# Hybrid projections: half of the modulation products move from VectorE to ScalarE and GpSimd, and their sums on TensorE one product later

## The reference, cut to what matters

```
def ada_modulation(cond, w, b):
    m = jax.nn.silu(cond) @ w + b
    return jnp.split(m, 6, axis=-1)
...
        sh1, sc1, gt1, sh2, sc2, gt2 = (t[:, None, :] for t in ada_modulation(c, ada_w[i], ada_b[i]))
        csh1, csc1, cgt1, csh2, csc2, cgt2 = ada_modulation(c_ctx, ada_w[i], ada_b[i])
```

## Time and profile before

| what | us |
|---|---|
| three timed runs | 3459.10, 3459.01, 3449.18 (median 3459.01) |
| the profiled execution | 3452.43 |
| its span, first to last instruction | 3450.6 |
| the stage in layer 0, first feature product to the end of the last row product | 43.07 to 294.61 |
| the stage in layer 1, the same | 495.49 to 743.30 |

### The profile page before, as it was taken

How to read it: one execution, slowest core, us unless ns; L and a number is a source line. 1 busy time by engine, 2 the same in 40 slices (tenths; PEclk the granted TensorE clock), 3 DMA queues, 4 the chain that set the end, 5 groups by cost and what they waited for, 6 DMA issues and landing times. The chain is left out here.

```text
span 3450.6 us, 72773 instructions
## 1 busy us (share of the span) xinstructions
PE 3102.1 (90%) x31974; PEld 1794.0 (52%) x31974; DVE 1645.8 (48%) x3491; ACT 784.3 (23%) x1863; POOL 313.3 (9%) x345
## 2 busy tenths in 40 slices
PE   6998999989799999599999979998888878698987
PEld 5854658646344565343333335557787765233332
DVE  3664635757464586411112154238887866322211
ACT  2103410125211372100000010136555541000000
POOL 0000000000011110000000000012332320000000
PEclk9998999999899999699999989999999998899999
DMA  6565125730311223599999922100000024699998
GB/s 181 148 206 160 26 80 143 206 111 26 112 64 43 74 67 122 199 371 391 389 389 392 351 85 73 43 1 5 4 5 4 5 109 180 253 409 410 417 410 350
DMA packets 136476, 605.34 MB, mean 175 GB/s; under 512 B 17409, under 2 KB 20033, under 8 KB 115553
## 3 DMA queue, kind: packets, MB, share of 16 engines
q1 hardware_dynamic: 131136, 583.38, 45.7%
q0 software_dynamic: 5024, 17.30, 2.1%
HBM read 578.50 MB, written 28.44 MB: 176 GB/s over the span
## 5 line engine op out<-in xcount | busy, mean ns | idle before, releaser
L2129 PE MATMUL psum<-ring,big 128*32 128x256 f32 (+1 forms) x2688 | 389.1, 496 | 19.6 <-issue 9.1
L2129 PE MATMUL psum<-front,big 128*32 128x256 f32 (+1 forms) x2384 | 320.0, 480 | 8.4 <-issue 4.2
L441 PE MATMUL psum<-h_uT,ring 128*128 128x264 f32 x1280 | 290.5, 387 | 0.0
L570 DVE SCALAR_TENSOR_TENSOR h_O<-h_O,cond_silu 128x512 f32<-128x512 f32 x336 | 227.1, 747 | 103.8 <-DMA h_O<-ada_w 103.8
L2129 PEld LDWEIGHTS psum<-ring,big 128*32 128x32 f32 (+1 forms) x2688 | 136.3, 124 | 262.0 <-issue 220.3
L441 PEld LDWEIGHTS psum<-h_uT,ring 128*128 128x128 f32 x1280 | 242.0, 190 | 46.5 <-issue 5.8
L2270 DVE TENSOR_TENSOR big<-big,psum 128x512 f32<-128x512 f32 (+1 forms) x48 | 28.8, 599 | 438.1 <-PE psum L2129 425.7
L2129 PEld LDWEIGHTS psum<-front,big 128*32 128x32 f32 (+1 forms) x2384 | 114.1, 122 | 206.0 <-issue 174.0
L2768 PE MATMUL psum<-ring,gates 64*64 64x128 f32 (+1 forms) x5120 | 171.7, 253 | 11.8 <-issue 10.0
L461 PE MATMUL psum<-ring,h_uT 128*128 128x512 f32 x384 | 169.3, 598 | 0.0
L2209 ACT ACTIVATE big<-psum 128x512 f32<-128x512 f32 (+1 forms) x48 | 23.5, 524 | 636.1 <-PE psum L2129 636.1
(11 more groups left out here) (454 smaller groups left out, 5118.0 us busy)
## 6 DMA issues: line engine op xcount, KB each, us to landing
ring<-moe_w SPq DMA_DIRECT2D x84, 2048.0 KB, 14.0
front<-moe_w SPq DMA_DIRECT2D x67, 2048.0 KB, 14.2
big<-moe_w SPq DMA_DIRECT2D x28, 2048.0 KB, 29.7
h_O<-ada_w SPq DMA_DIRECT2D x192, 256.0 KB, 2.9
ring<-w_in SPq DMA_DIRECT2D x16, 2048.0 KB, 13.1
X<-moe_w SPq DMA_DIRECT2D x13, 2048.0 KB, 12.5
ring<-na_w_qkv SPq DMA_DIRECT2D x6, 2048.0 KB, 8.1
ring<-w_out SPq DMA_DIRECT2D x4, 2048.0 KB, 9.2
```

The source lines that it names most:

```text
L441: last = nc.tensor.matmul(bank(k, pair_bank(q) + h, NH), w[:, a, f * P:(f + 1) * P], uT[:, a, halves[h]], start=a == 0, stop=a == KD - 1)
L570: nc.vector.scalar_tensor_tensor(into, ada(u), by, into, ALU.mult, ALU.add).then_inc(s.acc, 1)
L2129: last = nc.tensor.matmul(bank(k, b, r.width)[q * r.n:(q + 1) * r.n, :], rowsT[:, half * HALF_K + n, r.first:r.first + r.n], w[:, n, q * r ...
```

## The change

For the context's half, `weigh` on VectorE is dropped (it now does r = 0 alone, and `acc` counts one for a unit). ScalarE multiplies the unit's tile by the context's column into one of two small buffers (`ctx_part`, a free part of `X`), and GpSimd adds that buffer to the context's sum, or copies it there for the first unit of a chunk. ScalarE waits for the unit's load and, from the third unit on, for GpSimd's add two units back. It does so at a fixed place in its own queue: the units of place q are scaled before the copy-out of the product q+1, hence after the copy-out of product q. SyncE's load of the unit four later waits for VectorE and ScalarE. `mod_sum(n)` waits for VectorE's and GpSimd's counts, and `made` puts it after the product two places behind the last unit's, not one; `mod_out(n)` and the store move with it.

```diff
@@ mod_schedule
-                made.setdefault(q + 1, []).append(u // KD)
+                made.setdefault(q + 2, []).append(u // KD)
@@ hybrid_project
+    ctx_part = lambda u: k.X[:, LT + 1, u % 2 * CHUNK:(u % 2 + 1) * CHUNK]
@@ sync: load_unit
-                    sp.wait_ge(s.acc, 2 * (u - MOD_BUFS) + 2)
+                    sp.wait_ge(s.acc, u - MOD_BUFS + 1)
+                    sp.wait_ge(s.ctx_scaled, u - MOD_BUFS + 1)
@@ gpsimd
+            for u in range(MOD_UNITS):
+                n, a = u // KD, u % KD
+                into = acc(n)[:, 1, :]
+                pool.wait_ge(s.ctx_scaled, u + 1)
+                if a == 0:
+                    if n >= 2:
+                        pool.wait_ge(s.mod_summed, n - 1)
+                    nc.gpsimd.tensor_copy(into, ctx_part(u)).then_inc(s.ctx_acc, 1)
+                else:
+                    pool.wait_ge(s.ctx_acc, u)
+                    nc.gpsimd.tensor_tensor(into, into, ctx_part(u), ALU.add).then_inc(s.ctx_acc, 1)
@@ tensor: mod_sum
-                pe.wait_ge(s.acc, 2 * KD * (n + 1))
+                pe.wait_ge(s.acc, KD * (n + 1))
+                pe.wait_ge(s.ctx_acc, KD * (n + 1))
@@ scalar
+            def scale(u):
+                act.wait_ge(ada_here[u % MOD_BUFS], 16 * (u // MOD_BUFS + 1))
+                if u >= 2:
+                    act.wait_ge(s.ctx_acc, u - 1)
+                nc.scalar.activation(ctx_part(u), ada(u), ACT.Copy, scale=k.cond_silu[:, u % KD, 1:2]).then_inc(s.ctx_scaled, 1)
+
             for q, (kind, j) in enumerate(order):
+                for u in units[q - 1] if q else ():
+                    scale(u)
                 if kind == "mirror":
                     continue
@@ vector: weigh
-                for r in range(2):
-                    into, by = acc(n)[:, r, :], k.cond_silu[:, a, r:r + 1]
...
-                        dve.wait_ge(s.acc, 2 * u + r - 1)
-                        nc.vector.scalar_tensor_tensor(into, ada(u), by, into, ALU.mult, ALU.add).then_inc(s.acc, 1)
+                into, by = acc(n)[:, 0, :], k.cond_silu[:, a, 0:1]
...
+                    dve.wait_ge(s.acc, u)
+                    nc.vector.scalar_tensor_tensor(into, ada(u), by, into, ALU.mult, ALU.add).then_inc(s.acc, 1)
```

More of the change, by code:

```diff
@@ L353, in hybrid_project @@
     with ExitStack() as mem, stage(k, "product out_done mirror_out rope_step logits_out forget_act forget_dve lam_dve lam_act summed "
-                                      "ada_here0 ada_here1 ada_here2 ada_here3 gate_bias0 gate_bias1 acc mod_summed mod_out "
+                                      "ada_here0 ada_here1 ada_here2 ada_here3 gate_bias0 gate_bias1 acc ctx_scaled ctx_acc mod_summed mod_out "
                                       "row_stored0 row_stored1 cleared") as (block, s):
@@ L522, in _ @@
                 last.then_inc(s.out_done, 1)
+            for u in units[len(order) - 1]:
+                scale(u)
         @block.vector
@@ L563, in weigh @@
                 dve.wait_ge(ada_here[u % MOD_BUFS], 16 * (u // MOD_BUFS + 1))
-                for r in range(2):
-                    into, by = acc(n)[:, r, :], k.cond_silu[:, a, r:r + 1]
-                    if a == 0:
-                        nc.vector.tensor_scalar(into, ada(u), by, None, ALU.mult).then_inc(s.acc, 1)
-                    else:
-                        dve.wait_ge(s.acc, 2 * u + r - 1)
-                        nc.vector.scalar_tensor_tensor(into, ada(u), by, into, ALU.mult, ALU.add).then_inc(s.acc, 1)
+                into, by = acc(n)[:, 0, :], k.cond_silu[:, a, 0:1]
+                if a == 0:
+                    nc.vector.tensor_scalar(into, ada(u), by, None, ALU.mult).then_inc(s.acc, 1)
+                else:
+                    dve.wait_ge(s.acc, u)
+                    nc.vector.scalar_tensor_tensor(into, ada(u), by, into, ALU.mult, ALU.add).then_inc(s.acc, 1)
             def mod_out(n):
```

## The result

The changed kernel takes 3469.59 us in the median of 8 executions (3454.96 to 3473.48), the kernel before 3456.14 of 8 (3449.18 to 3459.10): a ratio of 1.0038 [1.0023, 1.0053], **slower by 13 us** where 3451.0 was forecast. The profiled execution took 3467.39 us, its span 3465.6.

What follows compares the result with a forecast made beforehand. TensorE was taken to bound both stages. From the profiled 3452.4 us, 5.5 of waits won and 1.0 left gave 3448.0, a gain of 4.5; off the executions' middle of 3455.7 that made about 3451, range 3444 to 3463.

Steps and rivals of the forecast that it cites:

- Moved: loads: Four-unit stretches: loads wait for ScalarE, chunk goes out at t0 + 4.5, copy-out ready at t0 + L + 12.4.
- the dear case: Late-unit path with GpSimd's add at 1.32 us and VectorE's operation at 1.51; the first two waits missed by 1.6 and 0.6.
- TensorE bounds, and only waits before sums count: Both stages: TensorE is the bound; its waits before sums cost 5.47 us together, all the change can win.
- ScalarE's added work is covered, late copies cost nothing: 96 scalings a layer at 0.63 us fit beside TensorE's products; a copy-out may be 14.4 us late before TensorE notices.
- GpSimd: 1.04 to 1.32 us an add: GpSimd's 84 adds and 12 copies: four take 4.2 to 5.3 us, covered by a row product of 7.0.
- VectorE's remaining half: VectorE's remaining operation may go from 0.69 to 1.51 us; 0.7 taken for the path, 1.5 kept for the range.
- L of 13.3 to 16.9: Time in us from a 2 MB chunk's issue to the arrival of the units queued behind it, from four measured pairs.
- Moved: the sum: Sum one product later, due 29.4 us after F15's end or 28.6 after F19's; TensorE waits only above L 17.0 or 16.2.
- With the dear values the ready time is 1.7 later: Copy-out behind late units with GpSimd's add at 1.32 us and VectorE's operation at 1.51: ready 1.7 us later.
- The end is free: End of each stage: the last sum, just before the last meta tile, costs nothing; 1.4 us a layer if stores land slowly.
- the wait only moves: Rival at the sums: TensorE waits one product later for as long as before; 3452 to 3459 us, chance 0.20.
- an engine becomes the bound: Rival at four-unit places: GpSimd (add above 1.78 us) or VectorE becomes the bound; about 3466 us at 1.90, chance 0.12.

Runs made afterwards that it cites:

- narrow_add2: The changed kernel with GpSimd's 84 adds a layer cut from 512 to 64 columns; median 3448.41 us, 0.9988 of the kernel before.
- vector_adds2: The changed kernel with GpSimd's copies and adds moved to VectorE, at the next place in the order; median 3461.66 us, 1.0023 of the kernel before.
- sum_later2: The kernel before with only its sums one product later, nothing moved to ScalarE or GpSimd; median 3452.87 us, 1.0004 of the kernel before.
- before again: The kernel before, unchanged, run once more for a second trace; median 3450.89 us, 1.0004 of the kernel before.
- after again: The changed kernel, unchanged, run once more for a second trace; median 3466.84 us, 1.0048 of the kernel before.
- out_first2: The changed kernel with VectorE's copy-out of a sum ahead of the same place's weighing; median 3459.70 us, 1.0033 of the kernel before.
- two_later_out_first: The changed kernel with sums one product later still and VectorE's copy-out ahead of the weighing; median 3456.95 us, 1.0022 of the kernel before.

## Why the prediction was wrong

**The step that failed is *Moved: loads*, in the part "the change, part by part"**: its term for working off the late units, from their arrival to the copy-out. I had the units of both places ahead of the copy-out, but let ScalarE, VectorE and GpSimd keep up with the loads, so that behind the last load there was one operation of 0.7 us, and came to 3.4 + 3.0 + 0.7 + 0.42 + 0.3, some 7.9 us. VectorE didn't keep up: its eight operations, 1.46 us each with GpSimd beside them, take 12.1 us with the copy-out (186.44 to 198.53). In the dear case I put 1.51 into the sum once, not eight times.

The rows above show which part was short. The fourth scaling ends at 190.29 + 0.72 = 191.01, 4.6 us after the units' arrival and not 3.4; with 3.0 for its load the last unit would be there near 194.0. At 193.94 VectorE still has three operations to do, 4.25 us and not 0.7. Had its operation stayed at 0.75 us, the same path would be 4.6 + 3.0 + 0.75 + 0.41 = 8.8 us. That is an estimate, but narrow_add2 comes to 9.0. By it some 3.3 of the 4.2 us that this term lacks are VectorE's slowing, and the rest the pace of GpSimd's adds, to which ScalarE is held. No run changes one without the other in this kernel, so the split is not shown.

The path of each kernel in layer 0, in us after the end of F15 (read as above: SyncE's chunk, VectorE's first late unit, the end of the copy-out, and TensorE's sum without its wait; the forecast's row has L = 16.9):

| kernel | chunk | L | worked off | copy-out done | sum due | wait |
|---|---|---|---|---|---|---|
| forecast | 4.5 | 16.9 | 7.9 | 29.3 | 29.4 | 0 |
| after | 5.8 | 16.4 | 12.1 | 34.3 | 30.1 | 4.34 |
| vector_adds2 | 4.6 | 15.8 | 9.8 | 30.1 | 30.1 | 0.20 |
| narrow_add2 | 3.7 | 15.5 | 9.0 | 28.1 | 30.0 | none |
| sum_later2 | 0.1 | 15.4 | 10.7 | 26.2 | 30.0 | none |

Of the forecast's miss of 5.0 us in "copy-out done", 4.2 are the working off, 1.3 the chunk (adds of 1.33 and scalings of 0.72, not 1.04 to 1.32 and 0.63), and L gives 0.5 back. Against sum_later2 the hybrid is 8.1 us later: 5.7 by the chunk, 1.0 by L, 1.4 by the working off. Narrowing the add takes back 6.1 of these and leaves 2.0, the net price of hanging the loads on ScalarE.

The second stretch, behind F19, inherits this. The pair of engines is still at the first one's units, so the chunk (205.30) goes out 11.0 us after F19's end instead of 4.5. The copy-out ends at 232.61, and the sum, due at 232.75 - 2.60 = 230.15 only because the first wait has already pushed it back, waits again.

By the prediction's other points:

- *TensorE bounds, and only waits before sums count.* Right. The floor was a little lower: 246.43, not 246.94, so that 6.5 us and not 5.47 could be won.
- *ScalarE's added work is covered, late copies cost nothing.* Right. The scaling took 0.72 for 0.63. F18's copy started at 190.92, 3.8 us after F18's end (half of 14.51 after 179.83), and TensorE did not notice.
- *GpSimd: 1.04 to 1.32 us an add.* Too low: 1.26 at least, 1.41 in the mean of layer 0 and of both layers. The row of 1.043 was the wrong neighbour; the one of 1.322 was right for an undisturbed add.
- *VectorE's remaining half: 0.7 for the path, "since GpSimd has its pauses when units are late".* Wrong, and the argument was upside down: late units arrive together, and behind them both engines have hardly a pause. The range of 1.5 was right for the place that counts.
- *L of 13.3 to 16.9.* Right: 16.4 and 15.2 (220.53 - 205.30).
- *Moved: the sum.* Two sums stand between t0 and the moved one, not one: it was due at t0 + 30.1, not 29.4, which is 0.7 us in the change's favour.
- *"With the dear values the ready time is 1.7 later."* By the prediction's own terms it is 2.0: 0.6 more for the chunk, 0.6 for the working off, 0.8 for VectorE. It changes no reading.
- *The end is free.* Right: TensorE's pause between the last meta tile and the next stage is 2.04 us after the change, 2.03 in sum_later2.
- *Rival "the wait only moves".* One of its conditions, the dear values, came true, and TensorE does wait one product later. But it let the waits stay as long as they were (3452 to 3459), and they grew. *Rival "an engine becomes the bound".* It named the right two engines, but asked whether they keep up with TensorE over a whole place (an add above 1.78 us). None has to: they need only be too slow once, in the queue behind a late transfer.

**What stays open.** The ratios put the loss at 13 to 17 us (I had expected 6 to 13 of after again), the stages at 9.4 and 9.9; some 4 to 7 us are not accounted for. The rest of the span varies by itself: behind the second stage it has 2707.3 us in before and 2716.8 in before again, 2718.3 and 2718.0 in the changed kernel's two traces, but 2708.4 in out_first2 and 2707.2 in two_later_out_first, which have the same work on ScalarE and GpSimd. This is the same stretch of layer 1's attention in before, before again and after (length; busy PE, PEld, DVE, ACT, POOL; clock, DMA share, GB/s):

```profile
743.30:850.00 106.70, 94.01 (x766) 67.72 (x767) 74.93 (x292) 64.33 (x191) 14.55 (x30) 0.95 0.07 24
```

```profile
735.20:847.00 111.80, 100.19 (x767) 71.96 (x764) 74.44 (x290) 64.46 (x191) 14.59 (x30) 0.86 0.07 22
```

```profile
747.30:858.00 110.70, 98.21 (x764) 70.69 (x765) 74.52 (x292) 64.38 (x191) 15.03 (x30) 0.90 0.08 23
```

The same matmuls keep TensorE busy for 94.0 us at a granted clock of 0.95 and for 100.2 at 0.86, and the kernel before stands at both ends. The first profile of before was the lucky one, so the difference of the two first spans, 15.0 us, overstates the change. What the change adds to the time outside its stages no run here has isolated.

## What to carry to other kernels

When an instruction is moved in a program, write down what stands ahead of it on every engine at its new place, and price the whole queue behind a late transfer, not the last instruction in it: engines that are idle half of the time still run at their worst, all at once, when late data come together. Work handed to GpSimd is not taken from VectorE if both touch SBUF in the same microseconds: here half of the operations went, and 6 to 9 of 146 us with them. And where a change has two parts, cost each alone: here the free one (the later sum) held all the gain in the stages, and the other spent more than that.

## What the runs showed of the hardware

- VectorE and GpSimd slow each other when both stream 128x512 float32 in SBUF. VectorE's multiply-add goes from 0.75 us to about 1.5 (four in 5.99 in the changed kernel), its multiply alone (L590, one tensor in) from 0.48 to 1.49, GpSimd's add from 1.26 to 1.81 at most (all in the changed kernel). The Trainium skill, "SBUF — State Buffer", section "SBUF: two separate sides", calls the shared port pair an exclusive lock that is held for a whole instruction. The trace agrees in kind and not in full size: one after the other the two would need 0.75 + 1.26 = 2.0 us a unit, and ScalarE's scalings, which follow GpSimd, come every 1.68 (188.61, 190.29).
- GpSimd's 128x64 adds in narrow_add2 take 0.32 us in the median, 0.36 in the mean and 0.88 at most, and VectorE's operation beside them stays at 0.75 in the median (0.93 at most).
- ScalarE's scaling in SBUF is not touched by either: 707 to 727 ns over 192 instructions of the changed kernel, with both others at work beside it.
